# Moving three high parts and two scale products of a two-block transformer's opening to GpSimd, and making the identity on the chip

## The reference

```python
def ada_params(cond, w_mod, b_mod):
    m = jax.nn.silu(cond) @ w_mod + b_mod
    return jnp.split(m[:, None, :], N_MOD, axis=-1)      # sh1, sc1, gt1, sh2, sc2, gt2

a_lat = rms_norm(x, g_norm_mix) * (1 + sc1) + sh1
ag = a_lat.reshape(B, L, FNET_GROUPS, FNET_GROUP_DIM)
f = jnp.fft.fft2(ag, axes=(1, 3), norm="ortho").real
h = x + gt1 * (f.reshape(B, L, D) @ w_fnet_out)
h = h + gt2 * conv_ffn(rms_norm(h, g_norm_ffn) * (1 + sc2) + sh2, w_up, w_conv, b_conv, w_down)
```

## Time and profile before

| | |
|---|---|
| median of 3 executions | 1523.39 us |
| lowest, highest | 1523.29, 1524.03 us |
| span of the profiled execution | 1521.2 us |
| median less the span | 2.2 us |
| instructions in the span | 26964 |
| TensorE busy | 98% of the span |
| VectorE, GpSimd, ScalarE busy | 69%, 67%, 42% |
| moved by the load queue in all | 172 MB |

### The profile page before, as it was taken

The page is one execution under the profiler, slowest core; times in us unless marked ns, Lnnn a source line. Parts: engine busy times, 40 slices in busy tenths (PEclk is TensorE's granted clock), DMA queues, the critical chain, the costliest instruction groups (busy, mean ns, idle before and its releaser), DMA issues.

```text
span 1521.2 us, 26964 instructions
## 1 busy us (share of the span) xinstructions
PE 1497.1 (98%) x9391; PEld 1355.7 (89%) x9391; DVE 1046.6 (69%) x1605; ACT 635.8 (42%) x1142; POOL 1013.0 (67%) x801
## 2 busy tenths in 40 slices
PE   7999999999999999999999999999999999999998
PEld 6998999998887899999888888888888999999897
DVE  7877777873428477766943667676457787777954
ACT  6543566650113355565122213232235565554442
POOL 4735877766666777776764647566466787776684
PEclk9999999999999999999999999999999999999998
DMA  9942333344233333445342232322232333333342
GB/s 374 404 154 73 102 104 97 101 153 160 97 111 87 94 112 116 121 126 152 96 123 69 84 109 83 118 74 83 70 97 84 97 111 103 103 110 87 95 114 69
DMA packets 236382, 179.30 MB, mean 118 GB/s; under 512 B 5393, under 2 KB 214673, under 8 KB 235921
## 3 DMA queue, kind: packets, MB, share of 16 engines
q1 hardware_dynamic: 235008, 171.98, 36.5%
q10 hardware_dynamic: 1296, 6.29, 1.2%
HBM read 173.01 MB, written 5.24 MB: 117 GB/s over the span
## 4 chain that ended last, share of the span: by engine, by line
PE 57%; DVE 5%; issue 3%; POOL 2%; ACT 1%; POOLq 0%; DVEq 0%; ACTq 0%
PE ps L1075 19%; PE ps L1078 19%; PE ps L1079 19%; POOL tmp L929 1%; POOL w_lo L947 0%; POOL tmp L938 0%; POOL rope_r L947 0%; DVE wide_lo L3130 0%; DVE ps L3116 0%; DVE act_lo L3124 0%; DVE ps L3117 0%; DVE ps L3118 0%; DVE tmp L3115 0%; PE ps L1509 0%; DVE gates_r L3124 0%
## 5 line engine op out<-in xcount | busy, mean ns | idle before, releaser
L1075 PE MATMUL ps<-act_hi,w_hi 128*128 128x256 f32 (+1 forms) x864 | 283.6, 328 | 3.0 <-ACT gates L1895 1.3
L915 POOL TENSOR_TENSOR w_lo<-raw,w_hi 128x1024 fp32r<-128x1024 f32 x110 | 274.7, 2497 | 9.2
L1078 PE MATMUL ps<-act_hi,w_lo 128*128 128x256 f32 (+1 forms) x864 | 280.1, 324 | 0.0
L1079 PE MATMUL ps<-act_lo,w_hi 128*128 128x256 f32 (+1 forms) x864 | 280.0, 324 | 0.0
L1075 PE MATMUL ps<-wide_hi,w_hi 128*128 128x512 f32 (+2 forms) x733 | 261.1, 356 | 1.5 <-POOL w_lo L915 0.6
L1078 PE MATMUL ps<-wide_hi,w_lo 128*128 128x512 f32 (+2 forms) x733 | 260.4, 355 | 0.0
L1079 PE MATMUL ps<-wide_lo,w_hi 128*128 128x512 f32 (+2 forms) x733 | 260.4, 355 | 0.0
L912 POOL TENSOR_TENSOR w_hi<-raw,zero 128x1 fp32r<-128x1 f32 x110 | 30.3, 275 | 260.7 <-PE ps L1075 259.8
L947 POOL TENSOR_TENSOR w_lo<-raw,w_hi 128x512 fp32r<-128x512 f32 x128 | 165.8, 1305 | 52.5 <-ACT w_hi L1643 51.9
L1075 PEld LDWEIGHTS ps<-act_hi,w_hi 128*128 128x128 f32 x864 | 165.1, 191 | 19.6 <-issue 3.2
L1078 PEld LDWEIGHTS ps<-act_hi,w_lo 128*128 128x128 f32 x864 | 165.2, 191 | 13.9 <-issue 1.4
(11 more groups left out here) (322 smaller groups left out, 3952.8 us busy)
## 6 DMA issues: line engine op xcount, KB each, us to landing
raw<-in_w_in SPq DMA_DIRECT2D x88, 512.0 KB, 4.2
gates<-in_w_mod_t SPq DMA_DIRECT2D x20, 1024.0 KB, 10.2
raw<-in_w_ffn_up SPq DMA_DIRECT2D x40, 512.0 KB, 3.9
raw<-in_w_ffn_down SPq DMA_DIRECT2D x22, 512.0 KB, 3.6
raw<-in_w_ff_gate SPq DMA_DIRECT2D x22, 512.0 KB, 3.8
raw<-in_w_ff_up SPq DMA_DIRECT2D x22, 512.0 KB, 3.8
raw<-in_w_r_out SPq DMA_DIRECT2D x16, 512.0 KB, 3.4
raw<-in_w_ff_down SPq DMA_DIRECT2D x16, 512.0 KB, 3.8
```

Of the source, the lines that this page charges most:

```text
L915: nc.gpsimd.tensor_tensor(w_lo[:, two, :], raw[:, slot, :], f32(w_hi[:, two, :]), SUB).then_inc(split_done, 1)
L1075: ins = mm(o, w, a, start=start, stop=False)
L1078: mm(o, wl, a, start=False, stop=False)
L1079: return mm(o, w, al, start=False, stop=stop)
```

## The change

The identity is made by GpSimd out of `ones` with one `affine_select`, and its load and the waits for it go. GpSimd also takes the high parts of `x` tiles 1, 2 and 3 from ScalarE, in the order of the list `POOL_HI`. Tiles 1 and 3 of the scale (c = 1) leave VectorE: GpSimd multiplies, ScalarE sums (`gain_sum`), with the bias divided by 1024 beforehand. ScalarE copies the silu row before the square sums of tiles 1 to 3. VectorE's list is put in another order: `x_lo(1)` stands ahead of the second pair of tables, and the shift tiles (c = 0) 4 to 7, of which three stood among `u_lo(4)` to `u_lo(7)`, stand behind them. The numbers that others wait for (`mod_done`, `shift_summed`) are counted anew. SyncE waits for both kinds of scale tiles before it loads over them.

```diff
+POOL_HI = [("table", 0), ("table", 1), ("x", 1), ("table", 2), ("table", 3), ("x", 2), ("x", 3)]
@@ SyncE: mod_chunk, opening
-                    if c != 1:
+                    if c == MOD_ORDER[1]:
+                        sp.wait_ge(mod_step, max(mod_done(1, k) for k in range(m, m + MOD_STEPS) if k in GAIN_DVE))
+                        if m + 1 in GAIN_POOL:
+                            sp.wait_ge(shift_summed, GAIN_POOL.index(m + 1) + 1)
+                    elif c != 1:
...
             dft_table(0)
-            sp.dma_start(identity, t["identity"]).then_inc(out_stored, 16)
             x_tile(1)
@@ GpSimd
             pool.wait_ge(consts_set, 5)
-            for k in range(TT):
+            nc.gpsimd.affine_select(identity, ones[:, :], pattern=[[-1, P]], compare_op=ALU.is_equal, fill=0.0, base=0,
+                                    channel_multiplier=1).then_inc(consts_set, 1)
+            def dft_hi(k):
                 pool.wait_ge(dft_loaded[k // 2], 16)
-                nc.gpsimd.tensor_scalar(wide_hi[:, S_DFT + k, :], dft_rows(k), 1.0, 0.0, MUL, ADD).then_inc(dft_hi_made, 1)
+                nc.gpsimd.tensor_scalar(wide_hi[:, S_DFT + k, :], dft_rows(k), 1.0, 0.0, MUL, ADD).then_inc(pool_hi_made, 1)
+            def x_hi(a):
+                pool.wait_ge(x_rstd, a + 1)
+                nc.gpsimd.tensor_scalar(xr_hi[:, a, :], x_tok[:, a, :], small[:, 2, a:a + 1], None, MUL).then_inc(pool_hi_made, 1)
...
+            pool.wait_ge(silu_row_copied, 1)
+            for m in GAIN_POOL:
+                pool.wait_ge(modw_loaded[m // MOD_STEPS], 16)
+                nc.gpsimd.tensor_tensor(modw[:, m, :], modw[:, m, :], rope_flat, MUL).then_inc(shift_product, 1)
             pool.wait_ge(dftd_hi_made, 1)
@@ TensorE
-            pe.wait_ge(consts_set, 5)
+            pe.wait_ge(consts_set, 6)
             pe.wait_ge(early_loaded, 16)
-            pe.wait_ge(out_stored, 16)
@@ ScalarE
+            def gain_sum(i):
+                m = GAIN_POOL[i]
+                act.wait_ge(shift_product, i + 1)
+                do(modw[:, m, :], modw[:, m, :], ACT.Identity, scale=early_cols("g_norm_mix", m, 1), bias=early_cols("b_mod", KT + m, 1),
+                   accum_out=gain_mix[:, m:m + 1]).then_inc(shift_summed, 1)
@@ VectorE
-            mod_tiles(1, range(6, 8))
-            u_lo(4)
-            u_lo(5)
-            mod_tile(0, 4)
-            u_lo(6)
-            mod_tile(0, 5)
-            u_lo(7)
-            mod_tile(0, 6)
+            mod_tiles(1, range(6, 8))
+            for m in range(4, 8):
+                u_lo(m)
+            mod_tiles(0, range(4, 6))
...
-                if m == 0:
-                    mod_tile(0, 7)
+                if m < 2:
+                    mod_tile(0, 6 + m)
```

More of the change, by code:

```diff
@@ L36 @@
 SHIFT_POOL = 4
+GAIN_POOL = (1, 3)
+GAIN_DVE = [m for m in range(KT) if m not in GAIN_POOL]
+GAINS = len(GAIN_POOL)
+POOL_HI = [("table", 0), ("table", 1), ("x", 1), ("table", 2), ("table", 3), ("x", 2), ("x", 3)]
 U_BANKS = 6
@@ L1657, in x_squares @@
                 do(small[:, 1, a:a + 1], small[:, 0, a:a + 1], ACT.Sqrt, scale=1.0 / D, bias=eps[:, :]).then_inc(x_std, 1)
-            def x_hi(a):
-                act.wait_ge(x_rstd, a + 1)
-                hi_of(xr_hi[:, a, :], x_tok[:, a, :], xr_hi_made, scale=small[:, 2, a:a + 1])
             x_squares(0)
-            x_hi(0)
+            act.wait_ge(x_rstd, 1)
+            hi_of(xr_hi[:, 0, :], x_tok[:, 0, :], xr_hi_made, scale=small[:, 2, 0:1])
+            act.wait_ge(silu_row_made, 1)
+            do(rope_flat, silu_psum, ACT.Identity).then_inc(silu_row_copied, 1)
             x_squares(1)
             x_squares(2)
-            x_hi(1)
-            act.wait_ge(silu_row_made, 1)
-            do(rope_flat, silu_psum, ACT.Identity).then_inc(silu_row_copied, 1)
             x_squares(3)
-            x_hi(2)
-            x_hi(3)
+            def gain_sum(i):
[3 more added lines that the diff above has]
+                   accum_out=gain_mix[:, m:m + 1]).then_inc(shift_summed, 1)
+            gain_sum(0)
             act.wait_ge(dftd_loaded, 16)
             hi_of(flat(wide_hi, S_DFTD), raw[:, 2, :], dftd_hi_made)
+            gain_sum(1)
             for m in range(2):
@@ L2354, in dft_lo @@
             def dft_lo(k):
-                dve.wait_ge(dft_hi_made, k + 1)
+                dve.wait_ge(pool_hi_made, POOL_HI.index(("table", k)) + 1)
                 hi, lo = (w[:, S_DFT + k, :] for w in (wide_hi, wide_lo))
@@ L2390, in _ @@
             link(stt(out=mod_bias(1), in0=mod_bias(1), scalar=1.0, in1=early_cols("g_norm_mix", 0, KT), op0=ADD, op1=MUL))
+            for m in GAIN_POOL:
+                link(ts(mod_bias(1)[:, m:m + 1], mod_bias(1)[:, m:m + 1], 1.0 / D, None, MUL))
             link(stt(out=mod_bias(4), in0=mod_bias(4), scalar=1.0, in1=early_cols("g_norm_ffn", 0, KT), op0=ADD, op1=MUL))
@@ L2396, in _ @@
             x_lo(0)
+            dft_lo(1)
             x_rstds(1)
-            dft_lo(1)
+            x_lo(1)
+            x_rstds(2)
             dft_lo(2)
-            x_rstds(2)
-            x_lo(1)
             dft_lo(3)
             x_rstds(3)
+            x_lo(2)
             dve.wait_ge(silu_row_copied, 1)
-            mod_tiles(1, [0])
-            x_lo(2)
+            mod_tile(1, 0)
             x_lo(3)
-            mod_tiles(1, range(1, 4))
-            u_lo(0)
-            u_lo(1)
+            mod_tile(1, 2)
             mod_tiles(1, range(4, 6))
-            u_lo(2)
-            u_lo(3)
+            for m in range(4):
+                u_lo(m)
             mod_tiles(1, range(6, 8))
-            u_lo(4)
-            u_lo(5)
-            mod_tile(0, 4)
-            u_lo(6)
-            mod_tile(0, 5)
-            u_lo(7)
-            mod_tile(0, 6)
+            for m in range(4, 8):
+                u_lo(m)
+            mod_tiles(0, range(4, 6))
             def shift_columns():
                 dve.wait_ge(u_made, KT)
-                dve.wait_ge(shift_summed, SHIFT_POOL)
+                dve.wait_ge(shift_summed, GAINS + SHIFT_POOL)
                 dve.wait_ge(mod_step, mod_done(0, KT - 1))
```

39 lines of the change are left out of this document (27 added, 12 removed).

## The result

| | before | after |
|---|---|---|
| median (8 executions each) | 1523.39 us | 1527.92 us |
| lowest, highest | 1523.12, 1524.03 us | 1527.44, 1528.60 us |
| span of the profiled execution | 1521.2 us | 1526.0 us |
| TensorE's column matmuls start | 48.52 us | 53.89 us |
| first `half_sums` | 92.97 us | 98.36 us |

The change makes the kernel slower by 4.5 us; the ratio is 1.0031, 95% interval 1.0021 to 1.0041. The prediction was 1523.2 us, range 1522.0 to 1524.4, with a chance of 0.03 for slower. It was wrong.

What follows compares the result with a forecast made beforehand. TensorE, busy 98%, sets the time, but opening gains of 1.6 to 4.1 us end at the first `half_sums`, paced by a full load queue. Only -0.2 us remains: 1523.39 to 1523.2 us, range 1522.0 to 1524.4.

Steps and rivals of the forecast that it cites:

- Identity: Opening: the load and its 6.7 us wait go, at most 1.1 us won; later loads land 0.2 us sooner.
- TensorE turns slow in its new wait: Rival, chance 0.08: idle ahead of the first `half_sums`, TensorE's clock falls, costing 1.2 us; 1524.4 us.
- High parts of x on GpSimd: Opening: each costs 1.2 to 1.6 us, `x_lo(1)` ends at 12.7 to 13.1, 2.1 us of waits shrink or vanish.
- Scale tiles: Opening: VectorE sheds two 1.3 us instructions, `u_lo(4)` to `u_lo(7)` come sooner; GpSimd's later shift products cost nothing.
- the rule of contention: Skill's rule that GpSimd contends with VectorE for SBUF; used to favour 1.6 over 1.2 us per high part.
- Shift tiles behind the last low part: Before the last `features` of the first kind: 0.9 us wait goes, but 2.5 us on VectorE may delay `f`.
- The dry queue: Rival, chance 0.03: a late shift column delays panel 3 and all loads behind; 1527 us for a column 9 us later.
- my rule: At panel 3's issue: each us that the shift column comes later than 57.5 goes straight to the end.
- Sum to the end: From the first `half_sums` on: TensorE's gain ends in a wait for ScalarE's square; only 0.16 us, rounded -0.2, remains.
- What would show it: Signs of right: identity wait about 3 us, `x_lo` and `u_lo` waits under 1 us together, second sums near 106.0.
- the marks of "wrong": First `half_sums` before 91 us, DMA share clearly under 1 between 50 and 60, or low clock over 4 us behind 92.
- The chance of 0.88 for no change: Whole kernel: forecast 0.76, slow clock 0.08 and change without effect 0.04, all within 0.2% of the old time.

Runs made afterwards that it cites:

- the kernel with constants: The changed kernel with GpSimd's three high parts of x taken with constants 1.0 and 0.0 instead of the column of reciprocals, output not the reference's: 1523.62 us.
- identity and order: The change with the high parts of x back on ScalarE and all scale products back on VectorE: 1522.36 us, ratio 0.9994; measured again 1522.45 us.
- the seven kernels with a late panel: The change, four variants with one or both GpSimd loans, and two of the kernel before with only SyncE's panel 3 held: 1523.62 to 1533.62 us.
- with two additions moved: The change without both GpSimd loans, plus GpSimd's sixth and seventh additions of squares ahead of its low part of w_up_first's third panel: 1520.38 us, ratio 0.9983.
- only x: The kernel before with only the high parts of x 1 to 3 moved to GpSimd: 1533.62 us, ratio 1.0066.

## Why the prediction was wrong

*Identity.* The wait fell to 3.0 us, as forecast. At most 1.1 us were to be won; the column came 0.61 us sooner, which is within the spread of kernels with one and the same opening, and a low clock behind the new wait of 2.77 us stands in the rows. That is the mechanism of my rival "TensorE turns slow in its new wait", at another place than I named. The one fall of the clock that I had cited for it, at 52 us, stands behind one-column matmuls and not behind a wait; falls behind waits are in the traces of these runs alone.

*High parts of x on GpSimd: the first step that failed.* I priced them from the earlier trace rows, half the width, at 1.2 to 1.6 us. They took 2.85 to 3.8 us. I had matched the engine and the width, but not the operand: with constants the same instruction took 1.05 to 2.02 us, and the kernel 1523.62 us. This term is mis-sized by a factor of two, and it put `x_lo(1)` to an end at 15.05 instead of 12.7 to 13.1. At my price the forecast would have stood: the kernel with constants, with both loans in it, is inside my range.

*Scale tiles: the second.* "So I cost this at nothing" looked only at GpSimd's own list. I had named the rule of contention a paragraph earlier, and applied it to GpSimd's price alone, never to VectorE's. The products run beside VectorE's low parts and delayed the column by 6.7 us where they were the only loan. Their price depends on what else is there: with cheap high parts both loans cost 2.9 us of column, and the change without the products is no sooner than the change with them (column at 54.22 against 53.89). The two tiles, 2.6 us, that VectorE shed bought at most that 0.3 us.

*Shift tiles behind the last low part.* The 0.9 us wait for `u_lo` went in the kernel of identity and order, to 0.3 us, and in the four executions with this order the column starts at 46.94 to 47.51, against 47.91 with the identity alone. In the change it stayed, at 0.88 and 0.34 us. I had feared VectorE's `f`: 0.4 us of waits, right in kind and small.

*The dry queue: the third, and the one that turned the delay into time.* I gave the column until 57.5 us, from the use of panel 3 at 57.51, and so booked 5.3 us of slack. That time contains the load's own time on the way: with the queue empty, in the kernel after, the panel is issued at 57.68 and lands 3.7 us later. By the seven kernels with a late panel the loads behind it are late by all that it goes out after 52.6 to 52.9 us, and before the change it went out at 52.56: the slack was 0.3 us at most. The time on the way does not explain all of it. In the kernel with constants the panel went out 1.5 us later than before and still landed at 57.45, but `w_up_first` was late by the same 1.5 us; what holds the loads between the two is not shown. In the kernel after the column was done at 57.60. By my rule that costs 0.1 us; it cost the loads 5.25. The chance of 0.03 rested on a column within 2 us of its old place, and so on the two prices above, and on this false slack. The 1527 us that this rival gave came near the measured 1527.92, but for a column 9 us later; it was 5.4 us later, so this nearness is luck. (For 3 us of loss the rule needs the column at 60.5 us, not at 60.7.)

*Sum to the end.* I held that the loads pace the root and the second sums, and that TensorE's own time does not matter. That chain is right as far as it was needed for a gain: identity and order, the change without its loans, has the first sums at 92.53, the root at 94.95 and the second sums at 105.98, where I forecast 92.4, 94.9 and 106.0. But I used it in one direction only. TensorE could come later by 1.1 us, since the first sums were over at 93.98 (not 94.2: the two rows overlap) and the root ran at 95.11; the load queue had no more than 0.3 us. A column 5.4 us late goes through both. And what cut the gain off was not the load at the head of the chain alone but the order of GpSimd's list behind it: with two additions moved, the sums ran at 91.41 with `w_up_first` only 0.5 us sooner than before.

*What would show it.* Two of the marks of "wrong" were there: the DMA share of 0.23 between 55 and 60, and waits for `x_lo` of 5.6 us besides the one for `x_lo(0)`, where under 1 was forecast. The chance of 0.88 for no change came from one belief, that the opening cannot reach the end; nearly all the unknown prices lay on the side of a loss, and none of them was let into the sum.

## What to carry to other kernels

A wait that swallows a gain says nothing of how much loss it can swallow: at the meeting point ask how much later each side could come, and price a delay and an advance apart. Before work is lent to GpSimd, see what VectorE does beside it, and price the instruction with its own operands (a factor for each partition is not a constant). Where the next load of an in-order queue is issued only after an engine's step, its slack is not the time to its landing: subtract at least the load's own time on the way, and see whether what stands behind it in the queue is late. Here 5.3 us became 0.3 at most.

## What the runs showed of the hardware

GpSimd's tensor-scalar on 128x1024 float32 took 1.05 us with two constants (a product and a sum) and 2.85 us with a factor for each partition from SBUF (a product alone), VectorE idle in both.

Where VectorE read two tiles from SBUF, VectorE and GpSimd stood still for each other's instructions. Two instructions of each engine in the kernel after show it, GpSimd's and then VectorE's:

```profile
24.45 3.39 POOL L891 TENSOR_TENSOR gates<-gates,rope 128x1024 f32<-128x1024 f32 x1
...
32.53 2.85 POOL L896 TENSOR_TENSOR mod_early<-mod_early,rope 128x1024 f32<-128x1024 f32 x1
```

```profile
22.65 2.93 DVE L2382 SCALAR_TENSOR_TENSOR wide_lo<-res,small,wide_hi 128x1024 fp32r<-128x1024 f32 x1
...
33.05 2.88 DVE L2420 SCALAR_TENSOR_TENSOR wide_lo<-tmp,wide_hi 128x512 fp32r<-128x512 f32 x1
```

`x_lo(3)` stands from 22.65 to 25.58. GpSimd's first product ends near 24.5, and what is left to 25.58 is 1.1 us, about what `x_lo` takes alone (1.27). The second product, begun at 24.45, takes 3.39 us, where the first took 2.41. `u_lo(1)` likewise ends at 35.93, some 0.6 us after the product that began at 32.53 is over. With one input from PSUM `u_lo` stays at 0.70 us beside the same products. The Trainium skill ("SBUF — State Buffer", SBUF: two separate sides) states just this, an exclusive lock held for the whole instruction. The trace agrees with it in these rows, but not in `x_lo(2)`: 2.07 us from 19.40, over at 21.47, inside GpSimd's high part of 19.28 to 22.12. The two other kernels with these high parts show the same 2.07 us (at 19.28 without the scale products, at 20.10 with only x).

The granted clock fell, mostly to the lower of its two levels, 1.2 GHz, behind some of TensorE's new waits and not behind others of the same length. It was 0.71 between 10 and 15 us in the kernel after, behind the wait of 2.92 us, and 1.00 between 20 and 25, behind the one of 3.40. With x back on ScalarE a wait of 3.72 us stands at the same place, and there the clock was 0.55. It differs between executions of the same instructions too: in the four profiles with the opening of identity and order it was 0.66, 0.70, 1.00 and 0.66 between 10 and 15 us, behind waits of 2.68, 3.38, 2.98 and 2.40 us.
